# Four transformer layers on one core: gate vectors broadcast by TensorE instead of by a DMA round trip

## The reference, cut to what matters

```python
mod = jnp.einsum('bd,dm->bm', c_act, w_mod[i]) + b_mod[i]
sh_a, sc_a, gt_a, sh_f, sc_f, gt_f = jnp.split(mod, N_MOD, axis=-1)
h = modulate(rmsnorm(x, g_mix_pre[i]), sh_a, sc_a)
...
x = x + gt_a[:, None, :] * rmsnorm(o, g_mix_post[i])
h = modulate(rmsnorm(x, g_ffn_pre[i]), sh_f, sc_f)
...
x = x + gt_f[:, None, :] * rmsnorm(y, g_ffn_post[i])
```

## Time and profile before

| | us |
|---|---|
| median of 3 runs | 1444.91 |
| lowest and highest | 1444.33 and 1452.72 |
| the profiled execution | 1444.91 |
| its span, first to last instruction | 1443.7 |
| TensorE busy, matmuls | 1328.7 |
| VectorE busy | 1052.5 |
| ScalarE busy | 736.2 |
| DMA, mean over the span | 221 GB/s |

### The profile page before, as it was taken

How to read it: one execution, slowest core, us unless ns; L and a number is a source line. 1 busy time by engine, 2 the same in 40 slices (tenths; PEclk the granted TensorE clock), 3 DMA queues, 4 the chain that set the end, 5 groups by cost and what they waited for, 6 DMA issues and landing times.

```text
span 1443.7 us, 21937 instructions
## 1 busy us (share of the span) xinstructions
PE 1328.7 (92%) x8728; PEld 1188.1 (82%) x8728; DVE 1052.5 (73%) x1628; ACT 736.2 (51%) x1233; POOL 105.2 (7%) x146
## 2 busy tenths in 40 slices
PE   4899899998889989999768999889999999999999
PEld 3798699986688779998656776579998799899987
DVE  6777788887648788789745774778887688666643
ACT  3655755542746575553644554564444454644442
POOL 0022000000014100000023141200000000000000
PEclk9999999999999999999979999889999999999999
DMA  8865567789467534668731512338888667356651
GB/s 339 339 234 206 189 246 257 285 309 344 164 247 272 195 130 180 266 231 310 267 120 45 207 59 113 117 136 308 308 305 305 257 233 278 128 223 232 233 196 55
DMA packets 48038, 320.03 MB, mean 222 GB/s; under 512 B 5360, under 2 KB 8000, under 8 KB 10560
## 3 DMA queue, kind: packets, MB, share of 16 engines
q1 hardware_dynamic: 47936, 318.63, 58.5%
HBM read 317.51 MB, written 1.10 MB: 221 GB/s over the span
## 4 chain that ended last, share of the span: by engine, by line
PE 67%; DVE 14%; ACT 7%; DMA 5%; issue 3%; POOL 2%; SPq 1%; DVEq 0%; ACTq 0%; POOLq 0%
PE mat L582 14%; PE mat L583 14%; PE mat L584 14%; PE mat L620 6%; PE mat L622 5%; PE mat L624 5%; DVE wlo L1480 4%; DVE raw L1498 3%; DMA raw<-in_down 2%; ACT whi L1047 2%; DMA raw<-in_mod 2%; POOL st L2068 1%; ACT tmp L1068 1%; PE mat L640 1%; PE mat L810 1%
## 5 line engine op out<-in xcount | busy, mean ns | idle before, releaser
L1480 DVE TENSOR_TENSOR wlo<-raw,whi 128x1024 fp32r<-128x1024 f32 x393 | 476.3, 1227 | 185.1 <-ACT whi L1047 183.3
L582 PE MATMUL mat<-hHL,whi 128*128 128x256 f32 x1864 | 532.9, 286 | 5.2 <-DVE tmp L1701 2.7
L583 PE MATMUL mat<-hHL,whi 128*128 128x256 f32 x1864 | 529.0, 284 | 0.0
L584 PE MATMUL mat<-hHL,wlo 128*128 128x256 f32 x1864 | 528.8, 284 | 0.0
L1047 ACT ACTIVATE whi<-raw 128x1024 fp32r<-128x1024 f32 x393 | 405.7, 1051 | 221.5 <-DMA raw<-in_down 84.6
L582 PEld LDWEIGHTS mat<-hHL,whi 128*128 128x128 f32 x1864 | 359.5, 193 | 11.5 <-DVE tmp L1701 3.0
L583 PEld LDWEIGHTS mat<-hHL,whi 128*128 128x128 f32 x1864 | 359.4, 193 | 0.1
L584 PEld LDWEIGHTS mat<-hHL,wlo 128*128 128x128 f32 x1864 | 359.3, 193 | 0.0
L1498 DVE SCALAR_TENSOR_TENSOR raw<-raw,cB 128x1024 f32<-128x1024 f32 x192 | 233.9, 1229 | 11.9 <-DMA raw<-in_mod 11.8
L620 PE MATMUL mat<-whi,aHL 128*128 128x512 f32 x352 | 114.9, 397 | 8.1 <-DVE wlo L1480 8.1
L622 PE MATMUL mat<-wlo,aHL 128*128 128x512 f32 x352 | 113.5, 393 | 0.0
(11 more groups left out here) (207 smaller groups left out, 1513.5 us busy)
## 6 DMA issues: line engine op xcount, KB each, us to landing
raw<-in_mod SPq DMA_DIRECT2D x96, 1024.0 KB, 5.6
raw<-in_qkv SPq DMA_DIRECT2D x48, 1024.0 KB, 7.2
raw<-in_gate SPq DMA_DIRECT2D x44, 1024.0 KB, 4.9
raw<-in_up SPq DMA_DIRECT2D x44, 1024.0 KB, 5.4
raw<-in_down SPq DMA_DIRECT2D x44, 1024.0 KB, 6.4
raw<-in_wo SPq DMA_DIRECT2D x16, 1024.0 KB, 4.9
gtb<-gates SPq DMA_DIRECT2D x8, 512.0 KB, 7.0
cB<-in_crow SPq DMA_DIRECT2D x3, 512.0 KB, 7.9
```

The costliest lines, as they stand in the source:

```text
L582: pe.matmul(o, wh[:, k, :], hH[:, k, :], start=(k == 0), stop=False)
L583: pe.matmul(o, wh[:, k, :], hL[:, k, :], start=False, stop=False)
L584: m = pe.matmul(o, wl[:, k, :], hH[:, k, :], start=False, stop=(k == KT - 1))
L1480: dve.tensor_tensor(out=wlo[:, n % NSPL, :], in0=raw[:, f % NRAW, 1024 * h:1024 * h + 1024], in1=whi[:, n % NSPL, :].bitcast(f32), op=ALU. ...
```

## The change

The round trip goes. Each gate is instead broadcast by TensorE: for column k of `modc` the weights are that column repeated 128 times, the moving operand is the identity, and the product is a 128 x 128 block in which every row is the column's 128 values. Four such matmuls fill one bank (a half of the gate, c = 0 or 1), and ScalarE copies the bank of 128 x 512 into `gtb`. `grow`, the DRAM tensor `gates`, and the semaphores `s_gate_out` and `s_gate_in` are gone; VectorE waits for `s_take` instead.

The places change too. On TensorE, gates (0, 2) and (2, 2) are made in wo of their layer, one half before tile 6 and one before tile 7; (0, 5), (2, 5) and (3, 5) in the down product, before tiles 10 and 12; (1, 2) after the forget gates' product, (1, 5) and (3, 2) in boundaries 3 and 6, both halves together, as before. The last three use banks 6 and 5; the others use bank 6 twice, and the second half waits for the copy of the first. On ScalarE, (0, 2) and (2, 2) are copied before the boundary; (0, 5), (2, 5) and (3, 5) right behind the high parts of down tiles 15 and 17; (1, 2) now stands ahead of a high part that it used to follow.

```diff
-GATES = [(l, p) for l in range(LAYERS) for p in (2, 5)]
-GATE_OUT, GATE_IN = {}, {}
-def _gate_loads():
...
+ROWS_BEFORE, ROWS_AFTER, ROWS_AT = {}, {}, {}
+ROWS_IN = {3: (1, 5), 6: (3, 2)}
+for _l in range(LAYERS):
+    for _p, _n in ((2, HALF["wo", _l, 2]), (5, HALF["down", _l, 10])):
+        for _c in range(2):
+            if (_l, _p) in ((0, 2), (2, 2)):
+                ROWS_BEFORE[HALF["wo", _l, 6 + _c]] = (_l, _p, _c)
+            elif _p == 5 and _l != 1:
+                ROWS_BEFORE[_n + 2 * _c] = (_l, _p, _c)
+                ROWS_AFTER[_n + 2 * _c + 5] = (_l, _p, _c)
+            ROWS_AT[_l, _p, _c] = len(ROWS_AT) + 1
...
-                if item in GATE_OUT:
-                    gate = GATES.index(GATE_OUT[item])
-                    sp.wait_ge(s_take, gate + 1)
-                    sp.dma_start(A["gates"][gate:gate + 1, :].rearrange("o (k p) -> (o k) p", p=P), grow[:, :]
-                                 ).then_inc(s_gate_out, 16)
-                if item in GATE_IN:
-                    l, p = GATE_IN[item]
-                    gate = GATES.index((l, p))
-                    sp.wait_ge(s_gate_out, 16 * (gate + 1))
-                    if l > 0:
-                        sp.wait_ge(s_row, ROW[2 * l - 1 + gate % 2, "b11"])
-                    sp.dma_start(gtb[:, gate % 2, :], A["gates"][gate:gate + 1, :].to_broadcast([P, D])
-                                 ).then_inc(s_gate_in, 16)
...
+        GATES_BY_TWO = [(1, 2)] + list(ROWS_IN.values())
+        def gate_rows(n):
+            if n in ROWS_BEFORE:
+                gate_row(*ROWS_BEFORE[n], 6)
-        def gate_row(l, p):
+        def gate_row(l, p, c, b):
             pe.wait_ge(s_mod, FIN_AT[l, p, rows_of(l, p)[0]])
-            pe.transpose(bank(6)[0:8, 0:P], modc[:, 6 * l + p, :], ident[:, :]).then_inc(s_gate_row, 1)
+            if ROWS_AT[l, p, c] > 1:
+                pe.wait_ge(s_take, ROWS_AT[l, p, c] - (2 if b == 5 else 1))
+            for j in range(4):
+                k = 4 * c + j
+                m = pe.matmul(bank(b)[:, P * j:P * j + P], modc[:, 6 * l + p, k:k + 1].to_broadcast([P, P]), ident[:, :],
+                              start=True, stop=True)
+            m.then_inc(s_gate_row, 1)
...
                 act.activation(whi[:, n % NSPL, :], raw[:, f % NRAW, 1024 * h:1024 * h + 1024], ACT.Copy).then_inc(s_hi, 1)
+                if n in ROWS_AFTER:
+                    gate_taken(*ROWS_AFTER[n])
...
-        def gate_taken(l, p):
-            gate = GATES.index((l, p))
-            act.wait_ge(s_gate_row, gate + 1)
-            if gate:
-                act.wait_ge(s_gate_out, 16 * gate)
-            act.activation(grow[:, :], bank(6)[0:8, 0:P], ACT.Copy).then_inc(s_take, 1)
+        def gate_taken(l, p, c):
+            g = int(p == 5)
+            act.wait_ge(s_gate_row, ROWS_AT[l, p, c])
+            if l > 0:
+                act.wait_ge(s_row, ROW[2 * l - 1 + g, "b11"])
+            act.activation(gtb[:, g, 512 * c:512 * c + 512], bank(6 - c if (l, p) in GATES_BY_TWO else 6), ACT.Copy
+                           ).then_inc(s_take, 1)
...
             else:
+                gate_taken(1, 2, 0)
+                gate_taken(1, 2, 1)
                 hi(1)
-                gate_taken(1, 2)
...
-            dve.wait_ge(s_gate_in, 16 * b)
+            dve.wait_ge(s_take, ROWS_AT[(b - 1) // 2, 5 if g else 2, 1])
```

More of the change, by code:

```diff
@@ L170 @@
 _mod_counts()
-GATES = [(l, p) for l in range(LAYERS) for p in (2, 5)]
-GATE_OUT, GATE_IN = {}, {}
-def _gate_loads():
-    for gate, after, then in (
-            ((0, 2), ("wo", 0, 6), ("gate", 0, 0, 0)), ((0, 5), ("down", 0, 14), ("down", 0, 18)),
[3 rows of a table removed]
-        GATE_OUT["w", CHUNK_OF[HALF[after]][0]] = gate
-        GATE_IN["w", CHUNK_OF[HALF[then]][0]] = gate
-_gate_loads()
+ROWS_BEFORE, ROWS_AFTER, ROWS_AT = {}, {}, {}
[9 more added lines that the diff above has]
+            ROWS_AT[_l, _p, _c] = len(ROWS_AT) + 1
 FETCHES = []
@@ L235, in build @@
         gtb = sb("gtb", [P, 2, D])
-        grow = sb("grow", [8, P])
         cB = sb("cB", [P, 3, D])
@@ L272, in build @@
         s_sq, s_pow, s_pow0, s_row = (sem(n) for n in ("s_sq", "s_pow", "s_pow0", "s_row"))
-        s_step, s_mod, s_take, s_gate_out, s_gate_in = (sem(n) for n in (
-            "s_step", "s_mod", "s_take", "s_gate_out", "s_gate_in"))
+        s_step, s_mod, s_take = (sem(n) for n in ("s_step", "s_mod", "s_take"))
         s_v, s_qk, s_o, s_oh, s_ol = (sem(n) for n in ("s_v", "s_qk", "s_o", "s_oh", "s_ol"))
@@ L575, in feature_product @@
                 n = first + i
+                gate_rows(n)
                 pe.wait_ge(s_lo, n + 1)
@@ L646, in tensor_boundary @@
             transposes(b, 0, 2, 3)
-            if b == 3:
-                gate_row(1, 5)
-            if b == 6:
-                gate_row(3, 2)
+            if b in ROWS_IN:
+                for c in range(2):
+                    gate_row(*ROWS_IN[b], c, 6 - c)
             for p in range(2):
@@ L726, in a_ready @@
                         pe.wait_ge(s_row, ROW[2 * l + 1, "b11"])
-                if l != 1:
-                    gate_row(l, 5)
                 token_product(HALF["down", l, 0], FT, token_order(FT, [1] * 9 + [2], 1 if l < 2 else 2), aH, aL, a_ready)
@@ L751, in tensor_causal @@
                 feature_product(HALF["fg",], 4, tiles=1)
-                gate_row(1, 2)
+                for c in range(2):
+                    gate_row(1, 2, c, 6 - c)
             at = 0
@@ L833, in tensor_stick_breaking @@
                 stick_scores(pair)
-                if pair == 4:
-                    gate_row(0, 2)
             elif pair > 0:
@@ L902, in tensor_differential @@
                     next(wo)
-                if u == 1:
-                    gate_row(2, 2)
                 if u == 2:
@@ L1139, in scalar_boundary @@
                 scalar_high(b, 1, p)
-            if b == 3:
-                gate_taken(1, 5)
-            if b == 6:
-                gate_taken(3, 2)
+            if b in ROWS_IN:
+                gate_taken(*ROWS_IN[b], 0)
+                gate_taken(*ROWS_IN[b], 1)
             hi(4)
@@ L1195, in scalar_program @@
                     hi(2 if l == 0 else 4)
+                if l in (0, 2):
+                    gate_taken(l, 2, 0)
+                    gate_taken(l, 2, 1)
                 scalar_boundary(2 * l + 1, early=int(l == 0))
@@ L1199, in scalar_program @@
                     act.preload_act_table_set("natural_log_exp_and_others")
-                if l != 1:
-                    gate_taken(l, 5)
                 hi(18)
@@ L1287, in scalar_stick_breaking @@
                 stick_logs(pair)
-                if pair == 5:
-                    gate_taken(0, 2)
             elif pair > 0:
@@ L1332, in scalar_differential @@
                                        ).then_inc(s_csq, 1)
-                if u == 2:
-                    gate_taken(2, 2)
                 if 0 <= u - 3 < len(UNIT_LIST) and UNIT_LIST[u - 3] in QKU:
@@ L2179 @@
     o = nc.dram_tensor("out_0_dram", (1, S, D), _mybir.dt.float32, kind="ExternalOutput").ap()
-    A["gates"] = nc.dram_tensor("gates", (8, D), _mybir.dt.float32, kind="Internal").ap()
     A["sums"] = nc.dram_tensor("sums", (H, S), _mybir.dt.float32, kind="Internal").ap()
```

## The result

| | kernel before | changed kernel |
|---|---|---|
| median of 14 runs each | 1446.07 us (1441.2 to 1452.72) | 1456.33 us (1453.26 to 1459.66) |
| the profiled execution, and its span | 1444.91, 1443.7 | 1458.6, 1457.4 |

The ratio is 1.0069, with a 95% interval of 1.0056 to 1.0083: 10.0 us slower. A second set of runs of the same kernel gave 1.0057 (1.0039 to 1.0075). The forecast was +5.4 us, 1450.3 us, with a range up to 1456.0.

A forecast was written before the change was run, and what follows sets the result against it. TensorE, busy 92% of the span, was taken to bound the kernel, with the round trips mostly hidden. Terms 1.6 - 2.2 + 2.3 - 0.5 + 0.9 + 3.3 = +5.4 us gave 1450.3 us, range 1441.0 to 1456.0.

The forecast's parts named there:

- (0,5): Layer 0's FFN gate, in the down product: new stand covered, broadcast 1.2 us off, clock gain 1.0; sum -2.2 us.
- The signs that the prediction named as right: Matmuls of 0.22 us, layer 0's square +1.8, `sums` +2.3, later down products +1.7, 3 us stand before tile 12, shorter later one.
- (0,2): Layer 0's mixer gate, in wo: two halves push the chain by 1.78, removed transpose saves 0.20; sum +1.6 us.
- (1,2): Layer 1's mixer gate, after the forget gates' product: both copies ahead of the high part delay the scan; +2.3 us.
- (1,5): Layer 1's FFN gate, inside boundary 3: work fits TensorE's stand and may bring the clock back; -0.5 us.
- The rival that goes by it: Clock comes back fully in layer 0's down product and boundary 3: +3.9 us, 1448.8 us; chance 0.18.
- (2,2): Layer 2's mixer gate, in wo: first half falls in a TensorE wait, only the second counts; +0.9 us.
- (2,5), (3,5): FFN gates in layers 2 and 3's down products: 1.78 each less 0.11 for the transpose; together +3.3 us.
- (3,2): Layer 3's mixer gate, inside boundary 6: both halves fit TensorE's 2.75 us stand; priced at zero.
- The stall isn't covered: Layer 0's down product ends later by its wait, wo's second half waits 0.6: +11.8, 1456.7 us; chance 0.12.
- Transfers on the path: Weight fetches behind each broadcast come earlier once it goes: 10.4 off, sum -3.8, 1441.1 us; chance 0.10.
- slow repeated weights: Matmuls with a repeated column as weights take 1.71 us a half everywhere: +12.8, 1457.7 us; chance 0.05.

## Why the prediction was right or wrong

**What bounds the kernel, and what the transfers are worth: right.** TensorE's added work counted, and eight round trips were worth about 2 us. That the kernel would be slower by under 1% held. The forecast of +5.4 was 4 us too low, and the time came out just beyond the range's upper end. The kernel before also ran 1.2 us above the profiled execution from which the sum started (1446.07 against 1444.91), and the changed kernel's runs in the first set lay 0.6 us above the pooled +9.4. Counted from 1446.07, +9.4 is 1455.5, inside the range: so the end of the range was passed by the 4 us of the terms and by scatter together. Two steps missed, and both lie past the point at which the prediction stopped reading the path: in (0,5) the gain was taken to outlast the product, and in layer 1's attention the clock's share was put at nothing. The signs that the prediction named as right came, the stands before tile 12 and before the product's end among them, but none of them looks behind the product's end, where the gain went.

**(0,2): mechanism right, size 0.5 too low.** The price of 0.89 was right for the first half. The second was 1.13 because it stood behind a wait, which the prediction granted as possible but took as nothing. So the stage is 2.13 longer, to 0.02, in each of the five traces, where the halves were priced at 1.78. The removed transpose stood ahead of this stage, and its 0.20 was no gain: with it, the second matmul of the next product begins 1.09 us behind the start of the eight matmuls ahead (114.75 and 113.66), and without it 1.08 (114.89 and 113.81).

**(0,5): the step that failed.** The prediction read the new stand as covered ("So the stall is covered") and added a gain from the clock, -2.2 in all. It took for granted that what TensorE gains by the end of the product is still there at the end of the stage. Up to the product's end it was right. The stage began 2.27 us later than before in the trace of the changed kernel (TensorE's first matmul of it), and its last two matmuls began at 371.89, where those of the kernel before began at 372.03: 2.4 us gained. Then the gain goes, by the first timeline above against that of the kernel before:

```profile
372.03 0.62 PE L624 MATMUL mat<-whi,aHL 128*128 128x512 f32 x2
372.49 0.82 PE L640 MATMUL mat<-ident,xn 128*128 128x128 f32 x6
374.49 0.70 PE L620 MATMUL mat<-whi,hHL 128*128 128x512 f32 x2 [1.18 <-issue]
...
384.10 0.73 PE L620 MATMUL mat<-whi,hHL 128*128 128x512 f32 x2 [3.04 <-DVE wlo L1480]
...
389.47 0.73 PE L620 MATMUL mat<-whi,hHL 128*128 128x512 f32 x2 [1.37 <-DVE hHL L1555]
```

With the 2.27 taken off, the value product began 1.1 earlier (375.68 against 374.49), its first matmuls behind the wait for weights 0.5 earlier (385.86 against 384.10), and the last row, at 392.71 in the changed kernel, 1.0 later. The five traces of each kernel say the same. The down product's last matmul begins 2.6 us earlier after the stage's start on average (65.6 against 68.2), a little more than was forecast. From there to the value product's first matmul it takes 2.6 to 3.6 us in the changed kernel, where all five traces before have 2.2: that is 0.95 lost. The value product takes 0.7 more, 30.3 against 29.6. The chain of the first trace shows what the first loss is: TensorE was first at the product's end, but the next layer's weights were not split, and VectorE came to the boundary at 368.84, behind them. The prediction stopped at TensorE's last matmul and didn't ask what was late next. The second goes with the clock: a low stretch stands in the value product in all five traces of the changed kernel (0.57 from 386 to 390 in the first), but in three of the five before too, so it is only in part the change's doing, if at all.

How much is lost goes with the new stand, which the prediction took as a fixed 3.0 us from one trace. It ends behind the transfer for tile 15, and in the eleven traces in which this gate is made the new way its length ran from nothing to 4.2. The stage against the mean of the kernel before (100.0 us), in order of the stand (traces of the experiments are among them; -3.7 and +1.8 are from kernels with transposes, which are cheaper by themselves):

| stand before the second half | traces | stage |
|---|---|---|
| none (copies placed earlier) | 3 | -2.3, -2.6, -3.7 |
| 1.67 to 2.10 us | 4 | -2.5, +0.4, -1.7, -2.9 |
| 3.16 to 4.18 us | 4 | 0.0, +1.5, +0.9, +1.8 |

So a gain of 2.3 and 2.6 is there where TensorE doesn't stand, and none behind a stand of over 3 us. That the stand eats it is likely and not shown: only the earlier copies change it alone, and nine traces without this gate's new work run from 98.4 to 102.8 us by themselves. In the changed kernel's five traces the stage is 0.9 shorter on average. The failed step costs the forecast 1.3 us, with a standard error of 1.0.

**(1,2): the product's side right, the stage not.** The high part and the scan moved by 2.2 as forecast, in each of the five traces. But the attention as a whole is 4.2 us longer (standard error 1.2), the largest miss of all stages, and taking the 2.2 away gave back 4.8 (2.1 to 7.5). The term had the added work alone, and nothing for the clock in the stretch that it moves. The other 1.9 us go with the clock: between 400 and 500 us the traces of the kernel before have 3.4, 17.1, 6.8, 3.4 and 3.4 us at the low level, those of the changed kernel 13.7, 10.2, 13.7, 13.7 and 6.8. That is a mean of 6.8 against 11.6, and 4.8 us at half the clock are up to 2.4 us of work. Whether the later scan causes this isn't shown: two traces without any gate's work have 17.1 and 6.8 us low and an attention longer than the first trace's by 4.4 and 2.4. Taken over all traces the miss is smaller: nine without this gate's new work have a mean of 78.4 us (75.8 to 81.0), eight with it as in the changed kernel 81.8 (79.9 to 83.6), 3.4 apart with a standard error of 0.9, though they come from several chips and kernels. The last pairs of traces were made to place the missing 2 us. They lean to theory B, that they lie in layer 1, and the interval still touches zero.

**(1,5), boundary 3: mechanism right, gain not kept.** The clock came back as forecast. The twelve transposes of the earlier trace rows, 2.82 us there, take 1.53 in four of the five traces of the changed kernel (2.82 in the fifth), although the sixteen new matmuls ahead of them ran partly at the low level:

```profile
521.65 2.54 PE L563 MATMUL mat<-ident,modc 128*128 128x128 f32 x16
525.23 1.53 PE L637 MATMUL mat<-ident,xn 128*128 128x128 f32 x12 [1.04 <-DVE xn L1579]
```

From the first of these transposes to the 144th matmul of the FFN, four of the five traces of the changed kernel are 0.64 us shorter than those before and the fifth is level: 0.5 on average, as forecast. They keep it up to the 744th, some 93 us into the stage. Then, in the FFN's last third, each of the five loses 0.2 to 0.9, which no trace before does. The chain goes there through a transfer of weights, their two parts and VectorE's L1973, for which TensorE waits. The transfer on the chain, and TensorE's stand on its timeline:

```profile
611.14 5.57 DMA raw<-in_up
```

```profile
620.79 0.39 PE L578 MATMUL mat<-hHL,whi 128*128 128x256 f32 x1 [0.17 <-DVE tmp L1973]
```

Over the whole stage -0.05 is left, where -0.5 was forecast. Again a gain of TensorE ends at the next wait for weights, but the fifth trace, which had gained nothing, loses 0.4 there too, and why the weights come later isn't shown. The Trainium skill says that activity releases the throttled state (TensorE: Matmul & The Clock Gate, Part 1: The HAM clock gate). This case's traces agree where a stand was filled (2.82 against 1.53, in four traces of five). The rival that goes by it, 1448.8 us, failed all the same: the time in boundary 3 came back and was lost behind it, and the same change made a stand elsewhere, with the clock at 0.57 behind it.

**(2,2), (2,5), (3,5): right.** +0.8, +1.77 and +1.76 for 0.9, 1.67 and 1.67. The transpose's 0.11 was gained: the product's 97th matmul begins 21.91 us behind the FFN's last one, where it was 22.01. So the two halves cost 1.85 together, against 1.78.

**(3,2), boundary 6: right.** It was priced at nothing. Its sixteen matmuls lie in the same stage as gate (2,5), which is 1.77 longer with both. The 0.4 that layer 3's wo, boundary 7 and FFN give back comes from a place that no gate's new work touches: in four of the five traces of the changed kernel the stretch at the low clock behind boundary 7, near 1250 us and in every trace of the kernel before, is gone, and there the stage is 0.7 shorter. It was not forecast, and its cause isn't shown.

**The sum.** +0.5 for (0,2) (0.35 in wo, 0.2 for the transpose), +1.3 for (0,5), +1.9 for layer 1's attention, +0.5 for boundary 3 and the FFN behind it, +0.2 for the two down products, -0.1 for (2,2); the stages priced at nothing give together -0.2 (+0.3, +0.7, and -0.3, -0.3, -0.2 and -0.4). That is 4.1, and 5.4 + 4.1 = 9.5. Of these only (0,2) and the two down products are known to a tenth. (0,5) and layer 1's attention, 3.2 of the 4.1, have standard errors of 1.0 and 1.2: the traces show where gains went, and how the 3.2 is shared between the two is not settled.

**The rivals.** "The stall isn't covered" came nearest in time (1456.7), by luck and another way: the new stand was covered, and the gain behind it was lost. Its other half, a wait of 0.6 in wo of layer 0, was 0.08. Transfers on the path fell by the two kernels without round trips, slow repeated weights by the 0.89 us. The range treated the terms' ends as the whole uncertainty. A lost gain in (0,5) was in the sum's dear end, +11.4, but nothing stood for layer 1's stages, which differ by up to 4.8 us between traces of one kernel and couldn't be judged from one trace.

**What stays open.** How much of the longer attention of layer 1, beyond the 2.2 us of the copies, is the change's doing; what sets the low stretches of the clock there and in the value product; why the weights come later at the end of layer 1's FFN; why the transposes gave back 6.6 us where 3.6 was expected; and what the one broadcast ahead of layer 0's last down weights is worth.

## What to carry to other kernels

Where a stage ends, follow the next stage's first wait as well: a gain that TensorE makes there is only kept if the next weights are already split. A copy placed one line ahead of the instruction on which a scan and sixteen broadcasts hang costs its own time and that of the matmuls it waits for, at full price. And before a sum of terms of 1 to 2 us is trusted in stages where engines stand by turns, look at a second trace of the same kernel: its scatter belongs in the range.

## What the runs showed of the hardware

- A group of eight recorded fp32 matmuls of 128x128x128 takes 0.89 us behind other matmuls and 1.13 behind a wait; with four recorded transposes of the same shape it is 0.44 and 0.62. Weights that are one column repeated 128 times cost nothing extra (0.89, as with L1010's changing weights).
- The granted clock differs between traces of the same code at the same place: 1.00 and 0.55 from 432 to 439 us in two traces of the kernel before. With it the length of that attention differs by 4.7 us. It happens on one chip too: the third and the fourth trace of the kernel before have 13.7 and 6.8 us at the low level between layer 0's down product and the end of layer 1's value product, and that stage takes 100.9 and 98.4 us.
- Stages in which TensorE is the path repeat to 0.02 us over five traces. The scatter of the whole span, 5.4 us over five traces of the kernel before and 8.0 of the changed one, comes mostly from the few stages in which it stands.
